# Inputs laid out by the host as their tiles are, in place of TensorE's transposes at the start and in the second layer

## What is computed

```python
h = rmsnorm(x, ln_g); proj = h @ w_in          # first layer, w_in is 1024 x 1696
...
x = x + sigmoid(x @ ple_w_gate[i]) * (p[i] @ ple_w_proj[i])   # p[i] is 512 x 256
...
ang = pos[..., None] * inv                     # rotary angles from the positions
...
wsm = where(causal, ws, 0)                     # spatial weights, 16 groups of 128 x 128
sv = einsum('gts,bcsgd->bctgd', wsm, v) + bs.T
```

## Time and profile before

| what | value |
|---|---|
| median of three runs | 1315.75 us (1315.42 to 1316.04) |
| profiled execution, first to last instruction | 1314.1 us; no other time is given for it |
| TensorE busy | 1295.6 us (99%), 6478 matmuls |
| VectorE, ScalarE, GpSimd busy | 758.1, 642.3, 343.7 us |
| the chain that ended last | TensorE 89%, VectorE 5%, issue 3%, ScalarE 2%, DMA 1% |
| moved by DMA | 104.66 MB, mean 80 GB/s |

### The profile page before, as it was taken

The page is one execution under the profiler, slowest core; times in us unless marked ns, Lnnn a source line. Parts: engine busy times, 40 slices in busy tenths (PEclk is TensorE's granted clock), DMA queues, the critical chain, the costliest instruction groups (busy, mean ns, idle before and its releaser), DMA issues.

```text
span 1314.1 us, 17855 instructions
## 1 busy us (share of the span) xinstructions
PE 1295.6 (99%) x6478; PEld 1086.5 (83%) x6478; DVE 758.1 (58%) x1209; ACT 642.3 (49%) x1164; POOL 343.7 (26%) x393
## 2 busy tenths in 40 slices
PE   7999999999999999999999999999999999999998
PEld 6998778788888888888888888889888888888986
DVE  5656889735652226898444653335467335578843
ACT  5379888624432325998244433414234234355632
POOL 2238877400000007773000000000000000668620
PEclk9999999999999999999999999999999999999999
DMA  5332100132232232001323333332332421421121
GB/s 192 84 108 65 45 25 15 53 106 97 81 99 97 99 99 73 17 0 32 112 97 93 87 93 97 96 97 64 87 110 82 135 96 49 129 65 49 33 64 65
DMA packets 70867, 104.66 MB, mean 80 GB/s; under 512 B 3476, under 2 KB 31368, under 8 KB 70664
## 3 DMA queue, kind: packets, MB, share of 16 engines
q1 hardware_dynamic: 69584, 99.44, 24.3%
q0 software_dynamic: 1088, 4.17, 1.1%
q10 hardware_dynamic: 120, 0.05, 0.0%
HBM read 101.55 MB, written 2.10 MB: 79 GB/s over the span
## 4 chain that ended last, share of the span: by engine, by line
PE 89%; DVE 5%; issue 3%; ACT 2%; DMA 1%; SPq 0%; DVEq 0%; POOL 0%; ACTq 0%; POOLq 0%
PE ps L496 24%; PE ps L498 23%; PE ps L497 23%; PE ps L700 3%; PE ps L1006 2%; PE ps L858 2%; PE ps L713 1%; PE ps L950 1%; PE ps L679 1%; PE ps L727 1%; PE ps L848 1%; DVE sp L2086 1%; PE ps L849 1%; PE ps L728 1%; DVE sp_l L2091 1%
## 5 line engine op out<-in xcount | busy, mean ns | idle before, releaser
L1689 DVE TENSOR_TENSOR w_lo<-stage,w_hi 128x1024 fp32r<-128x1024 f32 (+4 forms) x188 | 224.1, 1192 | 415.1 <-ACT w_hi L1108 414.9
L1108 ACT ACTIVATE w_hi<-stage 128x1024 fp32r<-128x1024 f32 (+4 forms) x188 | 191.0, 1016 | 457.2 <-PE ps L498 456.8
L496 PE MATMUL ps<-a0h,w_hi 128*128 128x512 f32 x512 | 204.5, 399 | 1.1 <-DVE q_lo L2273 0.8
L498 PE MATMUL ps<-a0h,w_lo 128*128 128x512 f32 x512 | 199.9, 390 | 0.0
L497 PE MATMUL ps<-a0l,w_hi 128*128 128x512 f32 x512 | 199.5, 390 | 0.0
L2375 POOL TENSOR_TENSOR small<-small 128x16 f32<-128x16 f32 (+2 forms) x14 | 32.3, 2311 | 388.0 <-DVE small L1767 284.4
L496 PE MATMUL ps<-w_hi,a0h 128*128 128x512 f32 (+1 forms) x320 | 121.9, 381 | 0.1
L498 PE MATMUL ps<-w_hi,a0l 128*128 128x512 f32 (+1 forms) x320 | 119.9, 375 | 0.0
L497 PE MATMUL ps<-w_lo,a0h 128*128 128x512 f32 (+1 forms) x320 | 119.8, 374 | 0.0
L496 PEld LDWEIGHTS ps<-a0h,w_hi 128*128 128x128 f32 x512 | 96.2, 188 | 20.5 <-DVE w_lo L1689 1.3
L498 PEld LDWEIGHTS ps<-a0h,w_lo 128*128 128x128 f32 x512 | 96.1, 188 | 20.6
(11 more groups left out here) (330 smaller groups left out, 2840.0 us busy)
## 6 DMA issues: line engine op xcount, KB each, us to landing
stage<-in_a_w_in SPq DMA_DIRECT2D x48, 512.0 KB, 3.7
stage<-in_ple_w_gate SPq DMA_DIRECT2D x16, 512.0 KB, 3.3
stage<-in_w_kv_shared SPq DMA_DIRECT2D x16, 512.0 KB, 3.6
stage<-in_sb_w_in SPq DMA_DIRECT2D x16, 512.0 KB, 3.7
stage<-in_a_w_out SPq DMA_DIRECT2D x16, 512.0 KB, 3.4
stage<-in_b_w_in SPq DMA_DIRECT2D x16, 512.0 KB, 3.7
stage<-in_mla_w_in SPq DMA_DIRECT2D x8, 512.0 KB, 3.9
stage<-in_sb_w_out SPq DMA_DIRECT2D x8, 512.0 KB, 3.4
```

The costliest lines, as they stand in the source:

```text
L496: pe.matmul(bank, wh, mh, start=start and not seeded, stop=False, skip_group_check=seeded)
L498: return pe.matmul(bank, wl, mh, start=False, stop=stop, skip_group_check=seeded)
L1108: act.activation(slab(w_hi[r % 2], L, nk, w), slab(stage[r % 4], L, nk, w), ACT.Copy).then_inc(S("hi_ready"), 1)
L1689: dve.tensor_tensor(slab(w_lo[r % 2], L, nk, w), slab(stage[r % 4], L, nk, w), slab(w_hi[r % 2], L, nk, w), ALU.subtract)\
```

## The change

The host passes `x` as its transpose (1024 x 512), `p` as 2 x 256 x 512, positions as 128 x 4, norm weights as 128 x 96 and the spatial weights as 128 x 2048 (source token by group and target token). They are loaded straight into `xT`, `p_T`, `pos_i`, `gains` and `ws_tok`. All 66 transposes of them are left out, with the copies from PSUM and the waits for them. The first loads are put in a new order, and in smaller pieces. `final_norm_g_2` becomes an input of its own. The diff, cut:

```diff
 @block.sync
-        sp_.dma_start(cst[:, :], ins["consts"][:, 0:ncst]).then_inc(S("cst_in"), 16)
-        sp_.dma_start(p_tok[:, :, :], ins["p"][0, 0].rearrange("(m p) c -> p m c", p=P)).then_inc(S("p0_in"), 16)
+        def p_rows(k):
+            sp_.dma_start(p_T[:, k, :], ins["p"][0, k * P:(k + 1) * P, :]).then_inc(S(f"p0_in{k}"), 16)
+
+        def x_rows(a, b):
+            for k in range(a, b):
+                sp_.dma_start(xT[:, k, :], ins["x"][k * P:(k + 1) * P, :]).then_inc(S(f"x_in{k}"), 16)
+
+        p_rows(0)
...
                 sp_.dma_start(stage[0][:, 0:nk, 0:w // 2], src[:, :, 0:w // 2]).then_inc(S("first_in"), 16)
+                p_rows(1)
                 sp_.dma_start(stage[0][:, 0:nk, w // 2:w], src[:, :, w // 2:w]).then_inc(loaded[0], 16)
...
-        for m in range(MB):
-            sp_.dma_start(x_tok[:, m, :], ins["x"][0, m * P:(m + 1) * P, :]).then_inc(S(f"x_in{m}"), 16)
+        x_rows(0, 4)
+        load(lin["mla_cq"].load0)
+        x_rows(4, KD)
+        sp_.dma_start(cst[:, :], ins["consts"][:, 0:ncst]).then_inc(S("cst_in"), 16)
...
 @block.tensor
-            if G == 1:
-                pe.wait_ge(S("x_new"), 4)
-            if G == lin["out1"].group0 + 1:
-                pe.wait_ge(S("ws_ok"), 4)
...
-                    if L.name == "mla_cq" and g == k == 0:
-                        pe.wait_ge(S("x_new"), 4 + n + 1)
...
+        linear("proj0")
         pe.wait_ge(S("cst_in"), 16)
-        pe.wait_ge(S("rows_in"), 16)
-        pe.wait_ge(S("pos_f"), 1)
-        pe.transpose(ps[7][:, 0:NG], gains_row[:, :], ident[0:NG, 0:NG])
-        pe.transpose(ps[7][:, NG:NG + MB], pos_f[:, :], ident[0:MB, 0:MB]).then_inc(S("gains_T"), 1)
...
-        extra_inputs(0)()
-        linear("proj0", before={1: x_columns(0, 4)}, second={1: x_columns(4, KD)})
...
-        linear("out1", before=on_the_way())
+        linear("out1")
...
 @block.scalar
+        def x_ready(r, k):
+
+            if r == 0:
+                act.wait_ge(S(f"x_in{k}"), 16)
+            else:
+                act.wait_ge(S("x_new"), 8 * (r - 1) + k + 1)
...
-        act.dma_start(gains_row[:, :], ins["gains"]).then_inc(S("rows_in"), 16)
-        act.dma_start(pos_i[:, :], ins["positions"][0].rearrange("(m p) -> m p", p=P)).then_inc(S("pos_in"), 16)
+        act.dma_start(gains[:, :], ins["gains"]).then_inc(S("rows_in"), 16)
+        act.dma_start(pos_i[:, :], ins["positions"]).then_inc(S("pos_in"), 16)
...
-            act.wait_ge(S("p_T"), k + 1)
-            act.activation(pTh0[:, k, :], ps[4 + k][:, :], ACT.Copy).then_inc(S("act_hi"), 1)
+            act.wait_ge(S(f"p0_in{k}"), 16)
+            act.activation(pTh0[:, k, :], p_T[:, k, :], ACT.Copy).then_inc(S("act_hi"), 1)
...
 @block.vector
         dve.wait_ge(S("pos_in"), 16)
-        dve.tensor_copy(pos_f[:, :], pos_i[:, :]).then_inc(S("pos_f"), 1)
-        dve.wait_ge(S("gains_T"), 1)
-        dve.tensor_copy(gains[:, :], ps[7][:, 0:NG]).then_inc(S("gains_ok"), 1)
-        dve.tensor_copy(pos[:, :], ps[7][:, NG:NG + MB]).then_inc(S("gains_ok"), 1)
...
+        dve.tensor_copy(pos[:, :], pos_i[:, :]).then_inc(S("pos_f"), 1)
...
-        linear("proj0", None, [lambda: stream("h_mla", 0, 4, take_x), lambda: stream("h_mla", 4, KD, take_x)])
+        linear("proj0", None, [lo_four("h_mla", 0, 4), lo_four("h_mla", 4, KD)])
...
-                dve.wait_ge(S("ws_T"), q + 1)
-                dve.tensor_tensor(wsT[:, 4 * q:4 * q + 4, :], ps[4 + q][:, :].rearrange("p (g t) -> p g t", g=4),
+                dve.tensor_tensor(wsT[:, 4 * q:4 * q + 4, :], ws_tok[:, 4 * q:4 * q + 4, :],
...
 @block.gpsimd
-        pool.wait_ge(S("x_in3"), 16)
+        pool.wait_ge(S("x_in7"), 16)
...
-            pool.dma_start(p_tok[:, :, :], ins["p"][l, 0].rearrange("(m p) c -> p m c", p=P)).then_inc(S("p_in"), 16)
+            pool.dma_start(p_T[:, :, :], ins["p"][l].rearrange("(k p) t -> p k t", p=P)).then_inc(S("p_in"), 16)
...
-        pool.dma_start(ws_tok[:, :, :], ins["a_ws_2"][0].rearrange("g t s -> t g s")).then_inc(S("ws_in"), 16)
+        pool.dma_start(ws_tok[:, :, :], ins["a_ws_2"].rearrange("s (g t) -> s g t", g=GROUPS)).then_inc(S("ws_in"), 16)
         pool.wait_ge(S("o2_read"), HEADS)
-        pool.wait_ge(S("ws_T"), 4)
+        pool.wait_ge(S("ws_ok"), 4)
```

More of the change, by code:

```diff
@@ L160, in build @@
     ones = keep("ones", [P, P])
-    gains_row = keep("gains_row", [NG, P])
     gains = keep("gains", [P, NG])
-    pos_i = keep("pos_i", [MB, P], I32)
-    pos_f = keep("pos_f", [MB, P])
+    pos_i = keep("pos_i", [P, MB], I32)
     pos = keep("pos", [P, MB])
@@ L331, in source @@
         return sum(max(0, min(s + 1 - first_item[name], n))
-                   for name, n in (("latent", 5), ("x0", 8), ("p1", 2), ("x1", 8), ("y", 16)))
+                   for name, n in (("latent", 5), ("x0", 8), ("x1", 8), ("y", 16)))
     ROUND = {"h_mla": 0, "h_kv": 1, "h_sb": 1, "h_g": 2, "h_bkv": 3, "h_bq": 3}
@@ L477, in _ @@
                 for r in range(L.load0, end_load(L.name)):
-                    load(r)
+                    if r != lin["mla_cq"].load0:
+                        load(r)
                     if r == 3:
@@ L787, in _ @@
             mla_step(h, h % 2, h // 2)
[L789 to L804, removed]
         pe.wait_ge(S("exp_done"), MB * HEADS)
@@ L920, in _ @@
         sb_values(HEADS - 1, 1, PAIRS - 1)
-        linear("out1", before=on_the_way())
+        assert lin["out1"].group0 % 2 == 0
+        linear("out1")
         linear("proj1")
@@ L1114, in hi @@
             if name in ROUND:
-                act.wait_ge(S("x_new"), 8 * ROUND[name] + k + 1)
+                x_ready(ROUND[name], k)
                 act.activation(h, xT[:, k, :], ACT.Identity, scale=gain(name, k)).then_inc(S("act_hi"), 1)
             else:
-                act.wait_ge(S("src_ready"), source(s))
+                if name == "p1":
+                    act.wait_ge(S("p_in"), 16)
+                else:
+                    act.wait_ge(S("src_ready"), source(s))
                 act.activation(h, src, ACT.Copy).then_inc(S("act_hi"), 1)
@@ L1170, in square @@
         def square(r, k):
-            act.wait_ge(S("x_new"), 8 * r + k + 1)
+            x_ready(r, k)
             if k >= 2 or r:
@@ L1208, in first_rows @@
         def first_rows():
-            act.wait_ge(S("gains_ok"), 2)
+            act.wait_ge(S("rows_in"), 16)
             for k in range(4):
@@ L1813, in _, with lo_four, do @@
         dve.wait_ge(S("pos_in"), 16)
-        dve.tensor_copy(pos_f[:, :], pos_i[:, :]).then_inc(S("pos_f"), 1)
-        dve.wait_ge(S("gains_T"), 1)
-        dve.tensor_copy(gains[:, :], ps[7][:, 0:NG]).then_inc(S("gains_ok"), 1)
-        dve.tensor_copy(pos[:, :], ps[7][:, NG:NG + MB]).then_inc(S("gains_ok"), 1)
[L1818 to L1828, removed]
+        dve.tensor_copy(pos[:, :], pos_i[:, :]).then_inc(S("pos_f"), 1)
+        def lo_four(name, a, b):
+            def do():
+                for k in range(a, b):
+                    lo(first_item[name] + k)
+            return do
         for k in range(2):
             dve.wait_ge(S("act_hi"), k + 1)
-            dve.tensor_tensor(pTl0[:, k, :], ps[4 + k][:, :], pTh0[:, k, :], ALU.subtract).then_inc(S("act_lo"), 1)
+            dve.tensor_tensor(pTl0[:, k, :], p_T[:, k, :], pTh0[:, k, :], ALU.subtract).then_inc(S("act_lo"), 1)
             split_to(k)
-        linear("proj0", None, [lambda: stream("h_mla", 0, 4, take_x), lambda: stream("h_mla", 4, KD, take_x)])
+        linear("proj0", None, [lo_four("h_mla", 0, 4), lo_four("h_mla", 4, KD)])
         def angles():
-            dve.wait_ge(S("gains_ok"), 2)
+            dve.wait_ge(S("pos_f"), 1)
             dve.wait_ge(S("cst_in"), 16)
@@ L2055, in rest_of_layer @@
             if l:
-                linear(f"out{l}", add_out(l), [nothing, lambda: stream("p1", 0, 2, extra_input(1)), nothing, meanwhile])
+                linear(f"out{l}", add_out(l), [nothing, lo_four("p1", 0, 2), nothing, meanwhile])
                 for k in range(3, KD):
@@ L2229, in q_rows @@
                                      bq_all[:, c:c + T].rearrange("p (i d) -> p i d", i=4), ALU.mult, ALU.add).then_inc(S(L.read), 1)
[L2231 to L2235, removed]
         def lo_and_norm():
@@ L2481, in _ @@
         root(nrm, MB, "nrm_in", 2, "nrm_ok")
-        pool.wait_ge(S("x_new"), 16)
+        pool.wait_ge(S("x_new"), 8)
         def kq_parts(pair, s, kq):
@@ L2653 @@
     gains += [np.reshape(inputs[name], -1) for name in ("a_ln_g_2", "a_ln_b_2")]
-    arrays["gains"] = np.concatenate(gains).reshape(NG, P)
+    arrays["gains"] = np.ascontiguousarray(np.concatenate(gains).reshape(NG, P).T)
+    arrays["x"] = np.ascontiguousarray(arrays["x"][0].T)
+    arrays["p"] = np.ascontiguousarray(arrays["p"][:, 0].transpose(0, 2, 1))
+    arrays["positions"] = np.ascontiguousarray(arrays["positions"][0].reshape(MB, P).T)
+    arrays["a_ws_2"] = np.ascontiguousarray(arrays["a_ws_2"][0].transpose(2, 0, 1)).reshape(P, GROUPS * P)
     arrays["consts"] = consts
```

19 lines of the change are left out of this document (9 added, 10 removed).

## The result

The changed kernel takes 1308.22 us (median of four runs, 1307.59 to 1308.8); the kernel before 1315.72 us in the same rounds. The ratio is 0.9943, with a 95% interval of 0.9931 to 0.9955. So it is faster, by 7.5 us where 10.05 were forecast, and 0.1 us above the end of the range. Run once more, in five further rounds, the same kernel gave 1308.27 us and 0.9941 (0.9927 to 0.9954).

What follows compares the result with a forecast made beforehand. TensorE was taken to bound the kernel almost everywhere, except at the start, where other things set the end. 7.45 us at the start plus 2.6 in out1 made 10.05, so 1315.75 became 1305.7 us, range 1303.9 to 1308.1.

Steps and rivals of the forecast that it cites:

- The first matmul: At the kernel's start: begins at 6.2 us instead of 8.66, with 6.05 to 6.7 by the two ends.
- The pace of TensorE: In proj0: eight slow matmuls in 3.58 us, then 40 at 0.2275 us, so proj0 ends at 18.9 us.
- ScalarE between the groups: From slab 2's split to the sums of squares: slab 3 split at 21.2 us, sums at 30.8, 7.45 us earlier.
- step 2: In mla_cq: TensorE arrives at 22.6 us and waits 0.5 us for slab 3's low part, ready at 23.1.
- step 4: In mla_cq: TensorE starts on slab 4 at 27.1 us, after another 0.3 us of wait.
- Rival one: Before the sums of squares: ScalarE's 1.38 us wait is taken by other work; 1307.0 us, chance 0.17.
- Rival two: Start of proj0: the clock rises at another point; 1307.2 us, or 1305.0 if after 2 us; chance 0.17.
- The slower rival: Between proj0 and mla_cq: TensorE waits for late constants; 1318.4 us or more, chance 0.02.
- the one of no effect: Start and out1: TensorE waits as long as it transposed; 1313.3 us or above, chance 0.02.
- out1: In the second layer: two stretches of only transposes, 0.80 and 1.67 us, go with their restarts; 2.6 us gained.
- start: Everything up to the sums of squares, which move from 38.26 to 30.8 us: 7.45 us gained.

Runs made afterwards that it cites:

- the small additions: GpSimd's additions two to seven of the squares cut from 512 columns to 8, against the changed kernel: 1305.32 us, ratio 0.9923.
- the transposes put back: 8 and 16 transposes of the identity, read by nobody, added to out1 of the changed kernel: 1311.14 us, ratio 0.9967.

## Why the prediction was wrong

It had the direction and the right terms, and its sum was 2.5 us too large.

*The first matmul*: 6.2 forecast, 6.36 measured. 0.2 us lost.

*The pace of TensorE*: the slow stretch was taken as eight matmuls. It was ten in the profile, and 7 to 13 in the others of this kernel and of its variants without the matmuls of ones. Two more cost 0.4 us. `mla_cq` began at 19.53, where 18.9 was said.

*ScalarE between the groups*: this is the step that failed. Slab 3's high part was forecast for 21.2, and with the 0.6 us of the two terms above it came at 21.85, as worked out. But I took VectorE's 1.86 us from there to the end of the low part over from before, and it took 4.1 (21.85 to 25.95). The duration of a low part was carried over as if it were a property of the instruction. In the kernel before, slab 3's began at 29.61, just ahead of the next addition. VectorE and GpSimd before:

```profile
25.76 1.58 DVE L1698 SCALAR_TENSOR_TENSOR a0l<-xT,gains,a0h 128x512 fp32r<-128x512 f32 x1
27.26 0.68 DVE L1820 COPY xT<-ps 128x512 f32<-128x512 f32 x1
```
```profile
25.48 2.99 POOL L2389 TENSOR_TENSOR acc<-acc,sq 128x512 f32<-128x512 f32 x2 [0.80 <-ACT sq L1175]
29.95 1.65 POOL L2389 TENSOR_TENSOR acc<-acc,sq 128x512 f32<-128x512 f32 x1 [1.47 <-ACT sq L1175]
```

The sign was there already: the low parts of tiles 4 and 5 took 1.28 and 1.58 us with an addition beside them, in place of 0.75, while a copy out of PSUM took 0.68 us beside one. Such copies stood between the low parts; the change took them out, and squares, low parts and additions came close together. So TensorE came to step 2 at 23.2 and began it at 26.0, 2.8 us later (2.62 of them by the list of waits), not 0.5; the 0.3 us forecast for step 4 did not come. That is 2.0 us net of the sum, and the small additions, which take 2.4 us off this wait, show it to be this.

*Rival one* (ScalarE's 1.38 us not recovered, 1307.0) was nearer in size, 1.2 us off, but wrong in its mechanism: from slab 2's split to slab 3's it is 7.5 us (14.35 to 21.85), 7.64 forecast, so ScalarE recovered them and VectorE lost more. *Rival two* (the clock) happened in part. *The slower rival* and *the one of no effect* did not happen: TensorE had no wait for the constants, and `out1` gave 2.6 us as worked out, which the transposes put back confirm.

The terms together: start 4.8 in place of 7.45, `out1` 2.6 in place of 2.6, and 0.9 us that nothing had forecast. Of these, 0.6 us are the two waits for later slabs that TensorE had at 513.9 and 958.1 us and that shrank or went; the forecast had left them as they were. Why VectorE is in time there now, and what the remaining steps of 0.1 us are, is not shown. The second profile has such steps at the same places, and 7.3 us of shift in all. The profiled run was the fastest of four, so the median shows 7.5 and not 8.3.

## What to carry over

When a change pulls the work of several engines closer together, don't carry durations over from the old trace: look for the same instruction at two durations, ask which engine was active beside the long one, and cost the new schedule with the long one wherever the two will meet. Where VectorE and GpSimd both read two operands from SBUF, put the instruction that TensorE waits for into a gap of the additions, or let the additions begin earlier; moving four instructions of ScalarE into its gap, and two of VectorE with them, was worth 2.4 us here, and with slab 3's split and the loads of the head gains moved too it was 3.3 us, almost half of the change itself. A gap of an engine ahead of a late one (2.85 us of ScalarE) is the first place to look for that.

## What was not expected of the hardware

The number of slow matmuls at the start moved between 7 and 13 from profile to profile with hardly any change in the code ahead of them (10 and 13 in the two profiles of the changed kernel itself), so up to 1.2 us at 0.2 us each, while the granted clock read 1.00 over the window shown. Matmuls of ones on an idle TensorE from 1.1 us on put the first product at the upper pace. A load of 128 rows of 16 bytes landed 3.3 to 4.1 us after its issue at 1.2 (VectorE's waits for the positions: 4.44 to 5.30), against 2.2 us for four rows of 512 bytes.
